# Splitting the Mamba layer's weights a chunk ahead, spreading dt's chain over Z, and letting DMA and TensorE take two products of the scan's core

## The chip, the cores and the metric

The program runs on one core of one Trainium2 chip. The metric is the device time in microseconds of one execution. Timed executions of the kernel before: 2147.05 us in the median of three (2145.24 to 2148.67).

## The reference

A stack of two layers over 256 latent tokens and 256 context tokens, width 1024, float32. Layer 0 mixes tokens with a Hyena long convolution, layer 1 with a bidirectional Mamba-2 scan; each mixer stands between two half-step SwiGLU feed-forward blocks. What the change touches is the Mamba mixer of layer 1:

```python
def project(h):
    zxbcdt = h @ in_w                       # z, x, B, C, dt side by side
    xbc = silu(dwconv_centered(xbc_part, conv_w, conv_b))     # 3 taps along the tokens
    dt = softplus(dt_part + dt_bias)
def ssd_chunked(xdt, da, bm, cm, init):     # per chunk of 128 tokens, per head
    a_cs = cumsum(a);  decay_in = exp(segsum(a))
    y_diag = einsum(cb, decay_in, x)
    states = ...                            # B^T (decay * x), carried over chunks
    y_off = einsum(cc, prev_states, exp(a_cs))
def finish(y, xs, z):
    y = (y + d_skip * xs) * silu(z)
    yg = y grouped in 8;  yg *= rsqrt(mean(yg^2) + EPS)
    return (yg * norm_w) @ out_w
```

Here `want_ctx` is false: the context tokens only supply the states with which the latent scan starts, in both directions. There are 32 heads of width 64 in 8 groups.

## The kernel before, in words

Channels lie on partitions, tokens on the free axis; latent and context tokens stand side by side (512 columns). Every weight product is done in three passes on TensorE (`mm3`, lines 1493 to 1495): high part of the weights by high part of the input, high by low, low by high. For that each 128x2048 chunk of weights is loaded to `raw[2]` (SyncE, `load`, line 411), its high part `wh[2]` is written by ScalarE (`split_hi`, line 558) and its low part `wl[2]` by VectorE (`split_lo`, line 883). Slots alternate: chunk n uses slot n % 2 of `wh` and `wl`, and its split waits until the chunk two before has been used (`w_used`); a raw slot is free when the low part of the chunk two before is done (`w_lo`).

The Mamba projection runs in this order. XB: 12 chunks of 256 channels for 512 tokens (x and B). DTP: one narrow chunk with dt, into bank 4. CP: 4 chunks for the 256 latent tokens (C). ZP: 8 chunks for the latent tokens (z). For XB and CP, `conv_chunk` (line 763) on ScalarE evicts two banks with the middle tap (line 770), VectorE adds the outer taps (`taps`, lines 1214 and 1216), ScalarE applies silu (line 776). In `conv_chunk` the split of the next chunk's weights comes first, then the wait for this chunk's matmuls, the evictions and the silus; so the following split stands behind these silus. In ZP the silu is the eviction (line 807). TensorE's waits between chunks are in `wide` (line 1763): `w_lo`, and banks free two chunks later; ZP waits for all of C's taps (line 1780).

dt's chain (softplus by a polynomial, cumulative sums, lines 1239 to 1294) is on VectorE: a first piece between DTP and CP (add, the 3.35 us reciprocal of line 1245), the rest in one block between CP and ZP, the last six small instructions after all of Z. Its results lie in `dts`, 64 partitions by 8 rows of 256, in the memory of `wh`/`wl`. ScalarE stores row 5 to `afscr` in HBM; SyncE reads it back, one head's two rows (forward and backward, 2 KB) broadcast to all partitions, into `afb[r]`.

After Z: TensorE turns B (`tb_mm`, line 1790), dt (line 1818) and the context's x (`turn_x`, line 1800); VectorE scales the turned x by rows of dt into `xtok` (line 1310); TensorE forms the states (line 1812); then the same turning for the latent x.

The core runs over 8 groups of 4 heads. ScalarE writes `csx[r] = exp(afb[r])` (line 840), GpSimd multiplies it by C (line 1480), ScalarE writes four 128-column exponentials into `ee[r]` (lines 844, 845, 849, 850), two of them from `dm`, which VectorE forms (`exponents`, lines 1333 and 1334); VectorE multiplies `ee[r]` by B.C (`products`, lines 1344 and 1345, semaphore `m_done`). TensorE adds the state part and four products for each pair of heads (lines 1864 to 1873), forms B.C of the next group (line 1839) and the sum of squares of the group two before (line 1847). VectorE gates a finished group (`gate_y`): two products with D (line 1357), then one with silu(z) (line 1361). ScalarE squares it (line 831) once `tt[2]` is free, which the sum of squares two groups before must release. Each engine takes this work in the order written in its block; only semaphores connect them. After the core come the group norm, the output product (MBOUT) and the last feed-forward block.

## Time and profile before

| What | Value |
|---|---|
| timed executions, median (lowest, highest) | 2147.05 us (2145.24, 2148.67) |
| profiled execution: time, and span from first to last instruction | 2147.36 us, 2145.5 us |
| TensorE busy, share of the span | 2001.8 us, 93% |
| VectorE, ScalarE, GpSimd busy | 1321.3, 686.0, 202.8 us |
| granted TensorE clock, mean | 0.971 |
| XB, one chunk on TensorE | 10.9 us |
| one tap of XB (128x510) / one modulation product (128x1024) on VectorE | 0.75 us / 1.2 us |
| raw weights of the Mamba projection, issue to landing, median | 5.4 us |
| issue of the two stores of dt's row (ScalarE's queue) | 0.8 us |

The slices of 2% of the span show TensorE at nine tenths nearly everywhere; the slices of the Mamba layer's middle are at seven and eight. A span is busy time, idle time that a wait ends, and matmuls at the lower clock level; the rows below show all three for the stretch from about 1510 to 1870 us, where the changed code runs.

### The profile page before, as it was taken

To read this page: it belongs to the slowest core of one execution; us is meant where nothing else is said; L and a number is where in the kernel's file an instruction comes from. 1 tells how busy PE (TensorE), PEld (TensorE's weight loads), DVE (VectorE), ACT (ScalarE), POOL (GpSimd) and SP (SyncE) were. 2 spreads that over 40 slices of the span, in tenths; PEclk is the share of its full clock that TensorE was granted. 3 is DMA by queue.
4 is the path that set the end of the run, shared out by engine and by line. 5 is a ranking of instruction groups with operands and counts; after the bars stand their busy time and mean duration, and the time that the engine had idled before them with its cause. 6 is when DMAs were issued, how large, how long until landed. Compare 5 with 4: busy or idle time off the path is not lost. (4 is left out here: it accounts for less than half of the span.)

```text
span 2145.5 us, 24954 instructions
## 1 busy us (share of the span) xinstructions
PE 2001.8 (93%) x10136; PEld 1672.0 (78%) x10136; DVE 1321.3 (62%) x1844; ACT 686.0 (32%) x913; POOL 202.8 (9%) x140
## 2 busy tenths in 40 slices
PE   5899999999989989999999999999899797698998
PEld 2688888878867868888887888888787784398998
DVE  6565546777857675554767565567765548845544
ACT  3422222232200232222224222222444335634442
POOL 1000000100023400000110000011000003340001
PEclk9999999999989999999999999999999898999999
DMA  8444435544520154442645444355432322444554
GB/s 322 152 159 155 137 106 183 165 139 135 179 76 1 41 165 148 139 155 83 201 153 171 138 152 143 104 173 165 147 118 89 118 84 74 123 133 152 186 155 141
DMA packets 274590, 298.25 MB, mean 139 GB/s; under 512 B 8912, under 2 KB 249136, under 8 KB 272688
## 3 DMA queue, kind: packets, MB, share of 16 engines
q1 hardware_dynamic: 270784, 285.44, 41.6%
q10 hardware_dynamic: 3696, 11.27, 1.4%
q8 instruction: 78, 1.28, 0.3%
q14 instruction: 32, 0.26, 0.0%
HBM read 290.31 MB, written 6.37 MB: 138 GB/s over the span
## 5 line engine op out<-in xcount | busy, mean ns | idle before, releaser
L1493 PE MATMUL banks<-xh,wh 128*128 128x512 f32 (+1 forms) x2120 | 782.3, 369 | 53.1 <-DVE xl L946 16.4
L1494 PE MATMUL banks<-xl,wh 128*128 128x512 f32 (+1 forms) x2120 | 777.0, 366 | 0.0
L1495 PE MATMUL banks<-xh,wl 128*128 128x512 f32 (+1 forms) x2120 | 776.4, 366 | 0.0
L883 DVE TENSOR_TENSOR wl<-raw,wh 128x2048 fp32r<-128x2048 f32 (+1 forms) x195 | 404.2, 2073 | 333.0 <-ACT wh L558 331.9
L558 ACT ACTIVATE wh<-raw 128x2048 fp32r<-128x2048 f32 (+1 forms) x201 | 349.6, 1739 | 644.6 <-PE banks L1495 562.9
L1493 PEld LDWEIGHTS banks<-xh,wh 128*128 128x128 f32 x2120 | 408.4, 193 | 124.5 <-issue 27.5
L1494 PEld LDWEIGHTS banks<-xl,wh 128*128 128x128 f32 x2120 | 408.4, 193 | 62.4
L1495 PEld LDWEIGHTS banks<-xh,wl 128*128 128x128 f32 x2120 | 407.8, 192 | 63.1
L1493 PE MATMUL banks<-gh,wh 128*128 128x512 f32 (+1 forms) x704 | 255.7, 363 | 2.9 <-DVE wl L883 1.6
L1494 PE MATMUL banks<-gl,wh 128*128 128x512 f32 (+1 forms) x704 | 255.2, 362 | 0.0
L1495 PE MATMUL banks<-gh,wl 128*128 128x512 f32 (+1 forms) x704 | 255.1, 362 | 0.0
L994 DVE TENSOR_TENSOR pp<-tt,banks 128x512 f32<-128x512 f32 (+1 forms) x88 | 50.7, 617 | 185.3 <-PE banks L1495 185.2
L1493 PEld LDWEIGHTS banks<-gh,wh 128*128 128x128 f32 x704 | 132.8, 189 | 24.5 <-DVE wl L883 2.2
L1494 PEld LDWEIGHTS banks<-gl,wh 128*128 128x128 f32 x704 | 132.8, 189 | 20.6
L1495 PEld LDWEIGHTS banks<-gh,wl 128*128 128x128 f32 x704 | 132.8, 189 | 20.4
L605 ACT ACTIVATE tt<-banks 128x512 f32<-128x512 f32 (+1 forms) x88 | 43.1, 542 | 271.0 <-PE banks L1495 271.0
L1430 POOL TENSOR_TENSOR acc<-acc,tt 128x512 f32<-128x512 f32 (+1 forms) x42 | 85.9, 2045 | 373.5 <-ACT tt L639 310.7
L1424 POOL MEMSET acc<- 128x512 f32 x6 | 3.2, 527 | 1176.0 <-DVE gl L974 931.4
L961 DVE SCALAR_TENSOR_TENSOR hT<-banks,mods,hT 128x256 f32<-128x256 f32 (+1 forms) x64 | 28.8, 481 | 108.2 <-PE banks L1495 108.2
L897 DVE SCALAR_TENSOR_TENSOR banks<-ada_rawo,cb 128x1024 f32<-128x1024 f32 x48 | 81.8, 1705 | 2.8 <-DMA ada_rawo<-in_ada_rest 2.8
L899 DVE SCALAR_TENSOR_TENSOR ada_rawf<-ada_rawf,cb 128x1024 f32<-128x1024 f32 x60 | 73.5, 1225 | 2.0
L897 DVE SCALAR_TENSOR_TENSOR banks<-ada_rawf,cb 128x1024 f32<-128x1024 f32 x60 | 73.7, 1228 | 0.0
(211 smaller groups left out, 1730.5 us busy)
## 6 DMA issues: line engine op xcount, KB each, us to landing
raw<-in_ffn_in SPq DMA_DIRECT2D x88, 1024.0 KB, 5.1
raw<-in_ffn_out SPq DMA_DIRECT2D x64, 704.0 KB, 4.8
ada_rawf<-in_ada_rest SPq DMA_DIRECT2D x60, 512.0 KB, 3.9
ada_rawo<-in_ada_rest SPq DMA_DIRECT2D x48, 512.0 KB, 4.0
raw<-in_mb_in_w SPq DMA_DIRECT2D x24, 1024.0 KB, 5.4
raw<-in_hy_in_w SPq DMA_DIRECT2D x12, 1024.0 KB, 5.2
afb<-decays SPq DMA_DIRECT2D x32, 256.0 KB, 3.1
raw<-in_mb_out_w SPq DMA_DIRECT2D x8, 1024.0 KB, 5.8
```

Source lines behind the costliest of these rows:

```text
L558: return act.activation(wh[n % 2][:, 0:cols], raw[r_slot][:, 0:cols], ACT.Copy).then_inc(w_hi, 1)
L605: act.activation(tt[u][:, 0:n], bank[u][:, 0:n], ACT.Silu).then_inc(gate_ready, 1)
L883: dve.tensor_tensor(wl[n_slot][:, 0:cols], raw[r_slot][:, 0:cols], wh[n_slot][:, 0:cols].bitcast(F32), ALU.subtract).then_inc(w_lo, 1)
L897: own(dve.scalar_tensor_tensor(banks[free][:].rearrange("p a n -> p (a n)"), pieces[i][:], half, cb0[:], ALU.mult, ALU.mult, accum_out=mod ...
L899: dve.scalar_tensor_tensor(pieces[i][:], pieces[i][:], half, c_ctx[:], ALU.mult, ALU.mult, accum_out=mods[layer][:, m, 1:2]).then_inc(ada_ ...
L961: ins = dve.scalar_tensor_tensor(x, bank[4 + um][:, w * L:w * L + L], mods[layer][:, i * 2 + (DT * k5 + um), w:w + 1], x, ALU.mult, ALU.add)
L994: dve.tensor_tensor(pp[(pi.q + u) % 2][:, 0:n], tt[u][:, 0:n], bank[2 + u][:, 0:n], ALU.mult).then_inc(p_ready, 1)
L1424: pool.memset(acc[:], 0.0).then_inc(acc_zero, 1)
L1430: pool.tensor_tensor(acc[:, 0:n], acc[:, 0:n], tt[um][:, 0:n], ALU.add).then_inc(acc_done, 1)
L1493: pe.matmul(dst, h, x_hi, start=start, stop=False)
L1494: pe.matmul(dst, h, x_lo, start=False, stop=False)
L1495: return pe.matmul(dst, l_, x_hi, start=False, stop=stop)
```

## The change

Splits: in XB, CP and ZP the split of chunk j+2 now comes right behind the evictions of chunk j, before the silus on ScalarE, and behind the taps of chunk j on VectorE (in XB before the modulation products). The waits for raw slots and for TensorE's banks are one chunk earlier to match; SyncE loads one chunk earlier at the joints between XB, DTP, CP and ZP. The loops of CP and ZP are written out.

dt: `dts` moves from the memory of `wh`/`wl` to that of `tt`, so that its rows may be written while Z's weights are in use. The chain is cut in pieces, which stand behind the low parts of ZP chunks 2 to 7. ScalarE's two exponentials and four stores stand behind the sixth eviction of Z; TensorE turns dt before ZP chunk 7.

After Z: TensorE turns x and B in mixed order.

Core: exp(af) is formed once for all heads by ScalarE (`dts` row 6), stored in `afscr[1]`, and SyncE loads it into `csx[r]` for each head, behind a wait for TensorE's use of the previous one (`cs_used`). ScalarE scales the latent x by D in place (`d_x`, `dx_done`), and TensorE adds it with an identity product per pair of heads; `gate_y` loses its two products with D.

The diff, cut to its core:

```diff
-        dts = at("dts", [P, 8, L], F32, o_w + 12 * KB)
+        dts = at("dts", [P, 8, L], F32, o_tt)
...
# SyncE
+            for j in range(4):
+                sp.wait_ge(w_lo, CP.w - 1 + j)
+                load(CP.raw + j, ...)
+            for j in range(8):
+                sp.wait_ge(w_lo, ZP.w - 1 + j)
+                load(ZP.raw + j, ...)
-            sp.wait_ge(af_st, 32)
+            sp.wait_ge(af_st, 64)
+            sp.wait_ge(tk_t, 1)
+            sp.wait_ge(w_used, ZP.w + 8)
             for g in range(GROUPS):
                 for r in range(HPG):
...
-                    sp.dma_start(afb[r][:], afscr[g * HPG + r].partition_broadcast(P)).then_inc(afb_in[r], 16)
+                    sp.dma_start(afb[r][:], afscr[0, g * HPG + r].partition_broadcast(P)).then_inc(afb_in[r], 16)
+                    if g:
+                        sp.wait_ge(cs_used, 2 * g - 1 + r // 2)
+                    elif r == 0:
+                        sp.wait_ge(dt_v, 4)
+                    sp.dma_start(csx[r][:].rearrange("p (a n) -> p a n", a=2),
+                                 afscr[1, g * HPG + r].partition_broadcast(P)).then_inc(cs_in[r], 16)
# ScalarE
-            def conv_chunk(pl, i, u, split, dst, n, t0):
+            def conv_chunk(pl, j, split, dst, n, t0):
+                act.wait_ge(w_used, pl.w + j + 1)
+                for s in range(2):
+                    ...  # evict with the middle tap
                 split()
...
+            def chunk_hi(pl, j, cols=CW):
+                r = pl.raw + j
+                split_hi((pl.w + j) % 2, cols, r % 2, r // 2 + 1, pl.w + j - 1)
+            for j in range(12):
+                conv_chunk(XB, j, lambda: (chunk_hi(XB, j + 2) if j < 10 else chunk_hi(DTP, 0, 8 * P) if j == 10
+                                           else chunk_hi(CP, 0)), lambda m: xb[:, :, m, :], NT, 0)
...
+            for j in range(8):
+                act.wait_ge(w_used, ZP.w + j + 1)
+                for s in range(2):
+                    act.activation(zsb[:, j * 2 + s, :], bank[2 * (j % 2) + s][:, 0:L], ACT.Silu).then_inc(z_free, 1)
+                if j < 6:
+                    chunk_hi(ZP, j + 2)
+                if j == 5:
+                    act.wait_ge(dt_v, 2)
+                    act.activation(dts[64:128, 4, :], dts[64:128, 3, :], ACT.Exp).then_inc(dt_e, 1)
+                    act.wait_ge(dt_v, 3)
+                    act.activation(dts[64:128, 6, :], dts[64:128, 5, :], ACT.Exp).then_inc(dt_e, 1)
+                    ...  # two stores of row 5, wait, two stores of row 6
...
+            def d_x(g):
+                for m in (2 * g, 2 * g + 1):
+                    act.activation(xb[:, 0, m, :], xb[:, 0, m, :], ACT.Copy, scale=dcol[:, m:m + 1]).then_inc(dx_done, 1)
+            act.wait_ge(tr_mm, 16)
+            d_x(0)
             for h in range(HEADS):
+                if r == 1 and g + 1 < GROUPS:
+                    d_x(g + 1)
-                act.activation(csx[r][:], afb[r][:].rearrange("p a n -> p (a n)"), ACT.Exp).then_inc(ex_done, 1)
# VectorE
+            for j in range(12):
+                for s in range(2):
+                    taps(XB, j // 2, j % 2, s, NT, 0)
+                if j < 10:
+                    chunk_lo(XB, j + 2)
...
+            chunk_lo(ZP, 2)
             own(dve.tensor_scalar(w, e, 2.0, None, ALU.add))
             own(dve.reciprocal(w, w))
+            chunk_lo(ZP, 3)
...              # three ops, polynomial terms 13 and 11
+            chunk_lo(ZP, 4)
...              # terms 9, 7, 5, 3, last product
+            chunk_lo(ZP, 5)
...              # dt, da, ones, two scans
+            chunk_lo(ZP, 6)
...              # rows 3, 0, 5, 1 of dts
+            chunk_lo(ZP, 7)
+                dve.tensor_tensor(zz, zz, bank[4 + (g - 1) % 2][:].rearrange("p (a n) -> p a n", a=2),
+                                  ALU.mult).then_inc(y_done, 1)
# GpSimd
-                pool.wait_ge(ex_done, h + 1)
+                pool.wait_ge(cs_in[r], 16 * g + 16)
# TensorE
+            for j in range(8):
+                pe.wait_ge(w_lo, ZP.w + j + 1)
+                ...  # bank free
+                if j == 7:
+                    pe.wait_ge(dt_v, 4)
+                    ...  # six transposes of dt
+                two_tiles((ZP.w + j) % 2, 2 * (j % 2), x0, n=L)
...
+            turn_x(0, 1, 0)
+            turn_b(0, 2)
+            turn_x(0, 1, 1)
+            turn_b(2, 4)
...
+                    m = 2 * g + p
+                    pe.wait_ge(dx_done, m + 1)
+                    pe.matmul(bank[4 + g % 2][:, p * L:p * L + L], ident, xb[:, 0, m, :], start=True, stop=False)
```

## Rows read from the trace of the kernel before

**Rows 1.** Stretches: length, busy us of PE, PEld, DVE, ACT, POOL, clock, DMA share, GB/s.

```profile
1655.00:1695.00 40.00, 28.80 (x203) 28.19 (x204) 24.26 (x29) 20.99 (x26) 0.00 (x0) 0.87 0.42 128
1695.00:1747.00 52.00, 48.02 (x375) 47.65 (x373) 22.95 (x19) 15.39 (x20) 0.00 (x0) 0.94 0.33 105
1747.00:1784.00 37.00, 28.23 (x151) 23.75 (x150) 23.16 (x45) 13.90 (x29) 3.81 (x3) 0.85 0.15 51
```

**Rows 2.** Timeline of TensorE, rows with idle time: start, duration, what, [idle, releaser].

```profile
1537.02 0.50 PE L1493 MATMUL banks<-xh,wh 128*128 128x512 f32 x1 [1.75 <-DVE wl L883]
...
1655.05 0.39 PE L1493 MATMUL banks<-xh,wh 128*128 128x256 f32 x1 [3.23 <-DVE wl L883]
1664.98 0.58 PE L1493 MATMUL banks<-xh,wh 128*128 128x256 f32 x1 [3.92 <-DVE wl L883]
...
1680.73 0.39 PE L1493 MATMUL banks<-xh,wh 128*128 128x256 f32 x1 [1.42 <-DVE wl L883]
...
1692.57 0.58 PE L1493 MATMUL banks<-xh,wh 128*128 128x256 f32 x1 [5.82 <-DVE tt L1216]
1704.99 0.58 PE L1493 MATMUL banks<-xh,wh 128*128 128x256 f32 x1 [3.98 <-DVE wl L883]
```

**Rows 3.** Timeline of ScalarE, then VectorE, at one chunk of C.

```profile
1673.59 1.02 ACT L770 ACTIVATE tt<-banks,vecs 128x256 f32<-128x256 f32 x2 [4.47 <-PE banks L1495]
...
1676.46 1.90 ACT L558 ACTIVATE wh<-raw 128x2048 fp32r<-128x2048 f32 x1
...
1678.39 2.29 DVE L883 TENSOR_TENSOR wl<-raw,wh 128x2048 fp32r<-128x2048 f32 x1 [2.29 <-ACT wh L558]
```

**Rows 4.** The same two timelines at chunks of Z.

```profile
1718.38 0.66 ACT L807 ACTIVATE zsb<-banks 128x256 f32 x2 [3.31 <-PE banks L1495]
1718.93 1.91 ACT L558 ACTIVATE wh<-raw 128x2048 fp32r<-128x2048 f32 x1
...
1720.87 2.29 DVE L883 TENSOR_TENSOR wl<-raw,wh 128x2048 fp32r<-128x2048 f32 x1 [3.47 <-ACT wh L558]
1726.63 2.29 DVE L883 TENSOR_TENSOR wl<-raw,wh 128x2048 fp32r<-128x2048 f32 x1 [3.47 <-ACT wh L558]
```

**Rows 5.** One group of the core (columns as rows 1), and the loads of afb.

```profile
1824.60:1834.40 9.80, 7.16 (x56) 3.86 (x56) 9.77 (x23) 7.38 (x22) 5.10 (x4) 1.00 0.35 110
DMA to landing us min/median/max: 3.0/3.1/4.5
```

**Rows 6.** The chain that ended last, one place of it a group apart.

```profile
1838.23 0.67 DVE mm L1344
...
1848.04 0.68 DVE mm L1344
```

**Rows 7.** Timeline of VectorE and ScalarE at dt's chain.

```profile
1659.15 3.35 DVE L1245 RECIPROCAL rs<-rs 64x512 f32<-64x512 f32 x1
1694.45 4.30 DVE L1263 SCALAR_TENSOR_TENSOR rs<-rs,tt 64x512 f32<-64x512 f32 x6
1656.58 1.28 ACT L791 ACT_TABLE_LOAD   x1 [3.91 <-DVE tt L1240]
```

**Rows 8.** Timeline of TensorE and VectorE between Z and the core.

```profile
1747.79 1.09 PE L1790 MATMUL banks<-small,xb 128*128 128x128 f32 x8 [0.75 <-ACT zsb L807]
...
1767.34 7.07 PE L1812 MATMUL banks<-xtok,btok 128*128 128x256 f32 x32
...
1774.96 9.66 DVE L1310 TENSOR_TENSOR xtok<-banks,tk 128x512 f32<-128x512 f32 x16 [4.32 <-PE banks L1800]
...
1784.67 2.07 PE L1839 MATMUL banks<-csb,xb 128*128 128x256 f32 x4 [3.77 <-DVE xtok L1310]
```

**Rows 9.** One line's instructions: count, duration ns min/median/max; and the last L1357.

```profile
L1333 DVE SCALAR_TENSOR_TENSOR dm<-afb,tkd x32: 339/572/998, 1769.5 to 1858.8; 128x128 f32<-128x128 f32 x32
L1361 DVE TENSOR_TENSOR zsb<-zsb,tt x8: 691/1005/1016, 1801.5 to 1866.4; 128x512 f32<-128x512 f32 x8
1865.45 0.87 DVE L1357 SCALAR_TENSOR_TENSOR tt<-xb,dcol,banks 128x256 f32<-128x256 f32 x2 [1.65 <-PE banks L1873]
```

More of the change, by code:

```diff
@@ L372, in build @@
         e_done = sem("e_done")
-        ex_done = sem("ex_done")
+        cs_in = [sem(f"cs_in{r}") for r in range(HPG)]
+        cs_used = sem("cs_used")
+        dx_done = sem("dx_done")
         cs_done = sem("cs_done")
@@ L773, in conv_chunk @@
-                for s in range(2):
-                    m = i * 4 + (u * 2 + s)
-                    act.wait_ge(conv_free, m + (pl.conv + 1))
+                    m = j * 2 + s
+                    act.wait_ge(conv_free, pl.conv + m + 1)
                     act.activation(dst(m), tt[t0 + s][:, 0:n] if n == L else
                                    tt[t0 + s][:].rearrange("p (a n) -> p a n", a=2), ACT.Silu).then_inc(cv_silu, 1)
-            def xb_pair(i, last):
-                for u in range(2):
-                    split = lambda: (split_hi(DTP.w, 8 * P, DTP.raw % 2, DTP.raw // 2 + 1, DTP.w - 1)
-                                     if last and u == 1 else next_hi(XB, i, u, 2) if i or u else None)
-                    conv_chunk(XB, i, u, split, lambda m: xb[:, :, m, :], NT, 0)
@@ L1245, in _ @@
             own(dve.reciprocal(w, w))
-            def c_pair(i, last):
-                for u in range(2):
-                    if last and u == 1:
-                        open_lo(ZP)
-                    else:
-                        next_lo(CP, i, u, 2)
-                    for s in range(2):
-                        taps(CP, i, u, s, L, 2)
-            steps(dve, 2, c_pair, own, 4)
-            z, z2, s_ = tt[0][hp, :], tt[1][hp, :], rs[hp, :]
+            chunk_lo(ZP, 3)
             own(dve.tensor_tensor(z, e, w, ALU.mult))
```

169 lines of the change are left out of this document (77 added, 92 removed).

## The prediction, made before the changed kernel was run

> **What bounds the kernel now.** I read the page first: TensorE is busy 93% of the span, so only stretches where it stands or runs slowly can give time back. The stretches of the Mamba layer [rows 1] show them: TensorE is busy 28.8 of 40 us in C (granted clock 0.87), 48.0 of 52 in Z (0.94), 28.2 of 37 in the turning and states part (0.85). TensorE's timeline, its rows with idle time before them [rows 2], then names the waits: 1.75 us at XB's third chunk, and in C and Z 3.23, 3.92, 1.42, 5.82 and 3.98 us, 18.4 together, all for VectorE (the low part of the weights four times, and once the last conv tap, L1216). After three of them a 128x256 matmul begins at 0.58 us instead of 0.39: the lower of the clock's two levels (1.2 against 2.4 GHz). Third, one chunk of C on ScalarE and VectorE [rows 3] shows why: eviction starts at 1673.59 and ends at 1674.61, but the split of the next weights starts at 1676.46, because the silus stand between and wait for the taps. The same places in Z [rows 4] have no silu between: chunk period 5.76 us, TensorE never idle. Last, the core: VectorE is busy 9.77 of 9.80 us [rows 5], and the chain of waits shows one loop of 9.81 us [rows 6].
>
> **XB.** The third chunk's low part no longer stands behind VectorE's first modulation product. New order: taps of chunk 0 until about 1527.4, low part 2.3 us to 1529.7; TensorE needs it at 1535.2. The 1.75 us wait goes; with the slower first matmul 1.9 us. The later chunks take 10.9 us on TensorE and had no waits; VectorE needs at most 0.8 (first eviction) + 3.0 (four taps) + 2.3 + 5.2 (four modulation products of 1.2 with their small reads), 11.3 of the 11.7 us until its next taps: covered by 0.4 us, and if that fails it eats the slack of the low part (over 4 us) first. The raw loads queue behind modulation loads on SyncE; weights land some 4 us before their split. Worth 1.9 us.
>
> **C and Z.** From the end of dt's matmuls (1655.05 - 3.23 = 1651.82) to the end of Z (1747.79 - 0.75 = 1747.04) are 95.2 us; twelve chunks at 5.76 are 69.1. What remains in the new order:
> - Start of C: last XB eviction, taps until 3.8 us after its start, low part 2.3: 6.1 us, against 5.3 us of dt matmuls. 0.9 us of wait remains, where there were 3.23.
> - In C, behind the end of a chunk: evictions 1.0 (0.9 before the next starts), high part 1.90, low part 2.29, handovers 0.15: 5.3 against 5.76 us [rows 3]. The four taps (1.9 us, from 0.6 on) end before the high part does. Cover 0.5 us. Silus and a 1.28 us table load fit behind the split on ScalarE.
> - In Z: 0.55 + 1.90 + 2.29 + 0.15 = 4.9 against 5.76 [rows 4]; cover 0.9 us.
> - dt's chain in pieces in Z's gaps on VectorE. The pieces: add and reciprocal 3.9 [rows 7]; three ops and two of the six polynomial steps (4.30/6 each) 3.3; four steps and one 3.6; five ops and scans 3.1; six small ops 2.1. With a low part of 2.3 these are 6.2, 5.6, 5.9, 5.4 and 4.4 in periods of 5.76. Added up in order, each low part still ends 0.3 to 0.6 us before TensorE wants it. This is the thinnest cover of the forecast: price if one piece is late, that lateness.
> - At Z's sixth eviction ScalarE takes two exponentials, four stores (0.4 each) and two table switches, 2 x 1.28 + 0.7 + 1.6 = 4.9 us. Queued behind: the silus of chunk 6, 2 us late. Nobody waits: chunk 7 uses the other banks, and the first turn into banks 0 and 1 comes 5.8 us later.
> - The six transposes before chunk 7 now lie on the path, 0.9 us (0.87 before, elsewhere on it).
> - Raw weights: a load is issued when the low part two chunks before ends; 5.4 us to land, 7.2 until the split. 1.8 us to spare.
> Sum 0.9 + 69.1 + 0.9 = 70.9; gain 24.3 us.
>
> A table switch stands in the trace as 1.28 us [rows 7], the exponential 0.02 us behind it. The Trainium skill (ScalarE: Activation LUTs, What ACT_TABLE_LOAD costs) counts 1.28 plus 1.38 us of drain for each switch and so speaks against two more of them in Z. By it the first exponential is 1.4 us later, dt's last product too, and TensorE waits about 0.9 us before chunk 7: gain 23.4 instead of 24.3.
>
> **Turning and states.** Now 37.6 us from 1747.04 to 1784.67. On the path: eight transposes 1.04 to 1.09 [rows 8], four such groups 4.2, then the last btok copy 0.7; four rounds of states at 3.5 (7.07 for two) with two more groups 2.1, 16.1; VectorE's sixteen products 9.66 with 0.7 before them. New: 4.9 + 16.1 + 10.4 = 31.4. The order gives 6.2 us: VectorE's first products start 1 us behind Z (8 us now), dt's tail and transposes are gone from here, and the slow transposes (16 in 3.7 us) with the waits that precede them. If the clock falls here anyway, 2 to 3 us of it are lost. SyncE's eight loads (4 row pairs, 4 exponentials) start at Z's end and must be there 16 us later: hidden. The scaling with D (ScalarE, after transpose 16) is done about 3 us before the core starts.
>
> **Core.** VectorE loses the two products with D (0.87 for both), ScalarE the 512-wide exponential (0.52 a head, 2.1 a group) against two copies with scale (0.7), TensorE gets two identity products (0.5 each). Yet the loop [rows 6] does not contain the products with D: products of head r=1 done, four rounds of TensorE (1.45), next B.C (1.06), sum of squares (0.97), square on ScalarE (0.7 with the handover), two exponentials, products of head 3: 5.0 us; then VectorE's products and exponents of heads 3, 0, 1: 3.9 us, and 0.9 us of stretching. That stretching is L1333, 0.34 us at least, 0.57 in the median, 1.00 at most [rows 9], each time while GpSimd's 1.27 us product runs. L1361, also with both inputs in SBUF, shows 0.69 to 1.02. In the new kernel GpSimd starts when its DMA lands, by my sum while VectorE is in its slack half of the loop; I take the 0.9 off. TensorE's extra 0.53 ahead of the pair puts it 0.25 us behind VectorE. New loop 9.81 - 0.9 + 0.25 = 9.15; seven intervals give 4.6. Bounds for the loop: 8.9 (TensorE not late) and 9.8 (stretching stays, its extra hidden). After the last head the products with D are on the path: 0.9. Together 5.5.
>
> **Loads in the core.** The four loads of a group become eight of 256 KB. Four keep the DMA engines busy 35% of 9.8 us [rows 5], 0.86 us each; eight are 6.9 of 9.15 us. One lands 3.1 us after issue, 4.5 where four were issued together. New on SyncE: each exponential's load waits for TensorE (cs_used), and the next head's row pair is queued behind it. The tightest is head 3's row pair: it now leaves 9.6 us into the loop, lands 12.7 to 14.1, and VectorE wants it at 12.9 with 1.4 us of slack. Hidden, just.
>
> **Sum.** 1.9 + 24.3 + 6.2 + 5.5 = 37.9. The profiled execution took 2147.36 (span 2145.5), 0.3 over the median: 2109.5 for it, 2109.2 for the median.
>
> **Rivals.**
> - The core keeps its 9.8 us: the loads let GpSimd collide with L1333 in the half of the loop without slack, or head 3's row pair is late. For: the stretching took 0.9 us in every group before, and the slack is thin. Against: by my times the collision moves. 2109.2 + 4.6 = 2113.8 (2112 to 2116). The Trainium skill (GPSIMD Engine Reference, Specifications) has GpSimd's SBUF interfaces shared with VectorE and colliding with VectorE instructions that have two SBUF inputs. L1333 keeps its two and GpSimd its 32 products, so that rule stands behind this rival; the rows of L1333 and L1361 agree with it.
> - Weights late in C and Z. For: covers of 0.3 to 0.6 us. If VectorE's pieces are 0.5 us longer, 3 to 4 us go in waits; and if such waits bring the lower clock at one or two chunks, 2.8 each (8.5 against 5.76): 2114 to 2121.
> - The loads bind the core in part: 1.1 us for each further load in a burst, (1.8 + 4.5 - 3.0)/3, makes eight 8.8 us, and with SyncE waiting in order 10 to 12: seven times 1 to 3, 2116 to 2130.
> - Slower than before: the row loads run one after another because SyncE's queue waits on cs_used between them. Gains outside the loop are 33.3 us, so it decides from 9.8 + 33.3/7 = 14.6 us a group, 1.8 us a load; at the full 3.1 us it would be 24.8 a group, 2220. Against: 4 loads landed within 6.3 us of the first issue.
> - Better: loop 8.9, C's first wait hidden, products of group 1 quicker: 2101 to 2104.
>
> **Chances.** Forecast 0.54 (own range 2104 to 2113), core unchanged 0.17, weights late 0.11, loads bind in part 0.08, slower 0.03, better 0.07. Range 2102 to 2121: the first three and half of the last. A change of 0.2%, 4.3 us, is what a measurement of this kernel can tell from none. Faster 0.95, same 0.02 (between the third and the fourth rival), slower 0.03.
>
> **What would show it.** C and Z: TensorE's waits between dt and the end of Z below 2 us, granted clock 1.00, twelve chunk starts 5.76 apart. VectorE's first xtok product about 1 us behind Z; core start 31.4 behind Z. In the core: distance of L1344 of head 3 from group to group 9.15, L1333 mostly at 0.34, TensorE's waits for m_done small. The prediction is wrong if low parts end after the chunk before them, if GpSimd's products still stretch L1333 on the loop, if SyncE's issues of row pairs come later than 10 us into a loop, or if the clock of the states part stays at 0.85.

## The result and the profile after

| | before | after |
|---|---|---|
| median of four executions | 2147.86 us (2145.24 to 2148.76) | 2110.43 us (2109.44 to 2111.57) |
| ratio, 95% interval | | 0.9834 [0.9819, 0.9849] |
| profiled execution, span | 2147.36, 2145.5 | 2109.44, 2107.6 |
| mean granted clock | 0.971 | 0.976 |

The changed kernel is 1.7% faster: 37.4 us by the medians, 37.9 by the two spans. The forecast was 2109.2 and a gain of 37.9. (The median of the kernel before, 2147.86, is that of four executions; the section on the chip has that of three of them.) The stretches of the Mamba layer in the changed kernel come first; the columns are those of [rows 1]: C with Z, turning and states, core.

```profile
1648.30:1718.90 70.60, 69.97 (x583) 69.77 (x584) 51.30 (x57) 37.75 (x49) 0.00 (x0) 1.00 0.50 151
1718.90:1749.30 30.40, 24.27 (x145) 20.81 (x143) 20.55 (x36) 11.17 (x22) 5.07 (x4) 0.92 0.24 77
1749.30:1836.30 87.00, 69.93 (x480) 37.15 (x480) 71.43 (x158) 52.40 (x149) 35.91 (x28) 0.93 0.66 194
```

Three numbers of the first row answer the forecast for C and Z: length 70.6 us (70.9), TensorE busy in nearly all of it, clock 1.00, where [rows 1] had 0.87 and 0.94. TensorE's timeline says the same; these are its rows with idle time from the start of XB to the core:

```profile
1509.22 0.77 PE L1511 MATMUL banks<-xh,wh 128*128 128x512 f32 x1 [2.91 <-DVE xl L967]
...
1522.87 0.50 PE L1511 MATMUL banks<-xh,wh 128*128 128x512 f32 x1 [0.53 <-DVE wl L953]
...
1648.93 0.39 PE L1511 MATMUL banks<-xh,wh 128*128 128x256 f32 x1 [0.64 <-DVE wl L904]
...
1723.24 3.72 PE L1847 MATMUL banks<-xtok,btok 128*128 128x256 f32 x16 [0.69 <-ACT btok L833]
...
1749.33 1.22 PE L1872 MATMUL banks<-csb,xb 128*128 128x256 f32 x2 [3.71 <-DVE xtok L1332]
```

The five waits of C and Z [rows 2], 18.4 us, have become one of 0.64, where 0.9 was forecast. XB's wait of 1.75 us is gone. The 0.53 us before XB's second chunk stood in the kernel before too (0.54).

Z's last matmul ends at 1719.0 (before at 1747.04). With it the 37.9 us between the spans divide so:

| part | before | after | gain | forecast |
|---|---|---|---|---|
| up to XB's first matmul (code not changed) | 1510.42 | 1509.22 | 1.2 | 0 |
| XB, dt, C, Z | 236.6 | 209.8 | 26.8 | 26.2 |
| turning and states | 37.6 | 30.3 | 7.3 | 6.2 |
| core, to the first matmul of the normalization | 88.8 | 87.0 | 1.8 | 5.5 |
| the rest | | | 0.7 | 0 |

So the sum fitted partly because errors cancelled: the core gave a third of what it was to give, and small gains elsewhere stood in for the missing 3.7: 0.6 and 1.1 more than forecast in the two parts above it, and 1.2 and 0.7 in code that wasn't changed.

**The core.** TensorE takes the four heads of a group in two pairs, p=0 and p=1. A loop is the distance from one start of p=1's products (first round L1904) to the next. The rows are p=1 and p=0 in turn, and the idle time in brackets is TensorE waiting for VectorE's products:

```profile
1779.37 0.65 PE L1904 MATMUL banks<-mm,xtok 128*64 128x256 f32 x4 [0.83 <-DVE mm L1367]
...
1782.74 0.65 PE L1904 MATMUL banks<-mm,xtok 128*64 128x256 f32 x4 [0.21 <-DVE mm L1367]
...
1788.76 0.65 PE L1904 MATMUL banks<-mm,xtok 128*64 128x256 f32 x4 [0.83 <-DVE mm L1367]
...
1792.69 0.65 PE L1904 MATMUL banks<-mm,xtok 128*64 128x256 f32 x4 [0.77 <-DVE mm L1367]
...
1798.70 0.65 PE L1904 MATMUL banks<-mm,xtok 128*64 128x256 f32 x4 [0.83 <-DVE mm L1367]
...
1803.61 0.65 PE L1904 MATMUL banks<-mm,xtok 128*64 128x256 f32 x4 [1.74 <-DVE mm L1367]
...
1809.63 0.65 PE L1904 MATMUL banks<-mm,xtok 128*64 128x256 f32 x4 [0.83 <-DVE mm L1367]
...
1812.76 0.65 PE L1904 MATMUL banks<-mm,xtok 128*64 128x256 f32 x4
...
1818.78 0.65 PE L1904 MATMUL banks<-mm,xtok 128*64 128x256 f32 x4 [0.83 <-DVE mm L1367]
```

These loops take 9.39, 9.94, 10.93 and 9.15 us (all seven: 8.47, 9.61, 9.39, 9.94, 10.93, 9.15, 8.53). The forecast's 9.15 is there where p=0 doesn't wait; the others are longer by p=0's wait of 0.21, 0.77 and 1.74 us. One place shows where such a wait comes from; VectorE (DVE) and GpSimd (POOL) side by side:

```profile
1788.62 0.35 DVE L1355 SCALAR_TENSOR_TENSOR dm<-afb,tkd 128x128 f32<-128x128 f32 x1
1788.70 1.41 POOL L1498 TENSOR_TENSOR tt<-tt,csb 128x512 f32<-128x512 f32 x1 [1.23 <-DMA tt<-decays]
1788.88 1.37 DVE L1356 SCALAR_TENSOR_TENSOR dm<-afb,tkd 128x128 f32<-128x128 f32 x1
1790.18 0.68 DVE L1366 TENSOR_TENSOR mm<-ee,banks 128x512 f32<-128x512 f32 x1
```

GpSimd's product starts as soon as its load has landed. The exponent instruction behind it (L1356, 0.34 us by itself) lasts 1.37 and ends at 1790.25, 0.14 after GpSimd's 1790.11. The product L1366, which reads one input from PSUM, is not stretched: 13 of the 32 run beside a GpSimd product, and none of the 32 takes over 0.69 us. The other two loops have such cases as well:

```profile
1779.23 0.81 DVE L1355 SCALAR_TENSOR_TENSOR dm<-afb,tkd 128x128 f32<-128x128 f32 x1
...
1798.57 1.33 DVE L1355 SCALAR_TENSOR_TENSOR dm<-afb,tkd 128x128 f32<-128x128 f32 x1
...
1801.28 1.35 DVE L1356 SCALAR_TENSOR_TENSOR dm<-afb,tkd 128x128 f32<-128x128 f32 x1
```

Between p=1's start, or just before it, and p=0's products the exponents are stretched by 0.47, 1.03 and 2.00 us in the three long loops (what 0.81, 1.37, and 1.33 with 1.35 have over 0.34), and TensorE's wait is 0.26 us less each time: that is the 0.25 us by which the forecast had TensorE behind VectorE. In the loop of 9.15 nothing is stretched there. The same sum, 9.15 and what the stretching exceeds 0.26 by, gives the four middle loops of this kernel and of three more below (quarter loads, split behind the silus, dt in one block), sixteen in all, within 0.04 us.

The groups of the exponents in the core, first before (L1333, L1334), then after (L1355, L1356):

```profile
L1333 DVE SCALAR_TENSOR_TENSOR dm<-afb,tkd 128x128 f32<-128x128 f32 x30 | 16.7, 557 | 0.0
...
L1334 DVE SCALAR_TENSOR_TENSOR dm<-afb,tkd 128x128 f32<-128x128 f32 x30 | 11.3, 376 | 0.0
```

```profile
L1355 DVE SCALAR_TENSOR_TENSOR dm<-afb,tkd 128x128 f32<-128x128 f32 x30 | 16.0, 532 | 2.7 <-DMA afb<-decays 2.6
L1356 DVE SCALAR_TENSOR_TENSOR dm<-afb,tkd 128x128 f32<-128x128 f32 x30 | 12.3, 410 | 0.0
```

Sixty instructions at 0.34 us are 20.4 us. Stretching of the exponents was 7.6 us before (16.7 + 11.3 - 20.4) and is 7.9 now, and 9.4 and 11.6 in two later kernels with the same code in the core: nothing of it went. It only changed form, fewer cases and longer ones: over 0.5 us 18 before and 12 after, over 1 us one (L1334, 1.40) and five. What did go is the stretching of the gate: L1361, with both inputs in SBUF, took 0.99 to 1.02 us in the seven cases beside a GpSimd product and 0.69 in the one without; L1378, which reads PSUM, takes 0.67 to 0.69 in all eight. New are 2.6 us of waits for row pairs. ScalarE's waits and the loads in the core:

```profile
ACT tt L846 <- PE banks L1880: 19.2, 7, 3.7
...
ACT ee L865 <- DMA afb<-decays: 3.0, 3, 1.4
```

```profile
afb<-decays SPq DMA_DIRECT2D x28, 256.0 KB, 4.7
```

The first row is the square of each group waiting for TensorE's sum of squares of the group before. A row pair lands 4.7 us after its issue where it was 3.1.

### The profile page after: what moved, and what is told of

Read it like the earlier page. It is cut to its first block and busy times, and to the rows that moved or that the text cites. A ratio compares the mean times of both kernels' runs of the same rounds, so it can differ in the third digit from the quotient of the medians.

```text
span 2107.6 us, 24932 instructions
## 1 busy us (share of the span) xinstructions
PE 1999.1 (95%) x10168; PEld 1667.9 (79%) x10168; DVE 1312.2 (62%) x1828; ACT 677.1 (32%) x899; POOL 203.0 (10%) x140
## 5 line engine op out<-in xcount | busy, mean ns | idle before, releaser
L1512 PEld LDWEIGHTS banks<-gl,wh 128*128 128x128 f32 x704 | 132.9, 189 | 20.4
```

The lines of the kernel that those rows point to most:

```text
L1512: pe.matmul(dst, h, x_lo, start=False, stop=False)
```

## Experiments

Each kernel is the changed kernel with the edit shown; each ratio is to the kernel before, run on the same chip. The first four ran on one chip, the next four on another, the last four on a third. Medians of before there: 2146.12, 2144.57 and 2145.11 us. The core falls into three parts: the start up to p=1's first products, the seven loops, and the end from p=1's last start to the norm. "Low until" is how long the granted clock stays at its lower level from the core's start on; "stretching" is that of the exponents.

| kernel | core | start | low until | seven loops | end | stretching |
|---|---|---|---|---|---|---|
| before | 88.8 | 12.0 | 9.0 | 67.2 | 9.6 | 7.6 |
| changed | 87.0 | 12.0 | 9.0 | 66.0 | 9.0 | 7.9 |
| exponentials back on ScalarE | 88.8 | 10.4 | 5.1 | 69.3 | 9.1 | 10.9 |
| D back on VectorE | 92.1 | 12.1 | 9.3 | 70.3 | 9.7 | 10.5 |
| both back | 89.1 | 12.2 | 9.5 | 67.2 | 9.7 | 7.6 |
| quarter loads | 85.1 | 10.5 | 5.2 | 65.6 | 9.0 | 6.5 |
| two square tiles | 85.1 | 10.4 | 5.3 | 65.9 | 8.7 | 11.6 |
| small product | 83.3 | 12.0 | 9.0 | 62.3 | 9.0 | 0.4 |
| squares and quarter loads | 82.1 | 10.4 | 5.1 | 62.9 | 8.7 | 9.0 |
| squares and row order | 85.6 | 12.2 | 9.4 | 64.6 | 8.8 | 13.7 |
| squares and gate | 81.7 | 10.5 | 5.1 | 62.5 | 8.7 | 6.9 |
| squares, order and gate | 81.0 | 12.1 | 9.4 | 60.0 | 8.8 | 9.9 |
| split behind silu (core as changed) | 87.6 | 10.5 | 4.2 | 68.1 | 9.1 | 11.6 |
| dt in one block (core as changed) | 86.4 | 10.4 | 5.1 | 67.0 | 9.0 | 9.4 |

Two things follow. The start takes 12.0 to 12.2 us or 10.4 to 10.5, with the clock low for 9.0 to 9.5 us or for 4.2 to 5.3; it doesn't follow the edits, so 1.5 us of a difference between two cores can be the clock alone. And the loops of three kernels with the same code in the core are 66.0, 67.0 and 68.1 us. (The two kernels with the old core repeat each other, 67.2 and 67.2.) So edits are compared by their loops, and a difference under 2 us there says nothing by itself.

Theories for the missing 3.7 us: **A**, the loop runs through sum of squares and square, and GpSimd's products stretch VectorE on it; **B**, eight loads a group, some queued behind TensorE, hold it back; **C**, VectorE's busy time bounds it. The expectations go by the core's whole length.

**Exponentials back on ScalarE.**

```diff
 # SyncE
-                    ...  # its wait for cs_used
-                    sp.dma_start(csx[r][:]..., afscr[1, g * HPG + r].partition_broadcast(P)).then_inc(cs_in[r], 16)
 # ScalarE
+                    act.wait_ge(head_mm, h - 3)
+                act.activation(csx[r][:], afb[r][:].rearrange("p a n -> p (a n)"), ACT.Exp).then_inc(ex_done, 1)
 # GpSimd
-                pool.wait_ge(cs_in[r], 16 * g + 16)
+                pool.wait_ge(ex_done, h + 1)
```

> Undoes one part of the core: the 512-wide exponential is again written by ScalarE from afb and GpSimd waits for it; SyncE loads only the four row pairs of a group (the two extra stores stay). Splits, dt's chain, turning and D on TensorE stay as changed. The core is measured from the first B.C matmul (L1872 in the changed kernel) to the first matmul of the group norm's broadcast: 88.9 us before, 87.0 after, 83.4 by my sum. Theory A (the loop through the sum of squares stays at 5.0 us, and GpSimd's products stretch VectorE's L1355 and L1356 on it, whoever releases them): the core is 86 to 88 us, the time within 2 us of the changed kernel's 2110.4. Theory B (eight loads of 256 KB a group hold the core back): the core falls to about 84 us, time about 2107.

Measured 2113.79 us, 0.9849 [0.9823, 0.9876]; core 88.8 us, row pairs land after 3.2 us again. That is outside both expectations: B's gain doesn't come, and A's 86 to 88 us and its 2 us around 2110.4 are missed too. The loops are 69.3 us, four of them 10.6, where the kernel before had 9.8. D on TensorE alone makes the loops 2.1 us longer than neither piece does (67.2, before and with both back), and only the short start hides it; the end is 0.6 us shorter.

**D back on VectorE.**

```diff
 # ScalarE
-            d_x(0)
-                    d_x(g + 1)
 # VectorE, gate_y
+                for mt in range(2):
+                    own.mark(dve.scalar_tensor_tensor(tt[3][...], xb[:, 0, m, :], dcol[:, m:m + 1], bank[4 + (g - 1) % 2][...],
+                                                      ALU.mult, ALU.add))
 # TensorE
-                    pe.matmul(bank[4 + g % 2][:, p * L:p * L + L], ident, xb[:, 0, m, :], start=True, stop=False)
```

> Undoes the other part of the core: the products with D are again two VectorE instructions in gate_y, no copies with scale on ScalarE and no identity products on TensorE; exponentials still by DMA. Theory A (the products with D are off the loop except behind the last group, where they cost 0.9 us; TensorE's identity product puts it 0.25 us behind on the loop): core 87 to 89 us, time 2110 to 2113. Theory C (VectorE's busy time bounds the core): the core goes up by 8 times 0.9, to 94 us, time about 2117.

Measured 2115.82 us, 0.9859 [0.9834, 0.9884]; core 92.1 us, VectorE busy 82.32 of it, granted clock 0.87 (0.93 in the changed kernel). It lies between the two expectations. The loops are 70.3 us: exponentials by DMA without D on TensorE are 3.1 us worse than neither piece.

**Both back.** The two diffs above together.

> Both parts of the core's change are undone (exponentials on ScalarE, products with D on VectorE); projections, dt's chain, turning and states stay as changed. If the core of the changed kernel is only worth what the two traces differ by (1.8 us), the core is 88.8 us and the time 2112.2 (2111.5 to 2113). If one half of the core's change needs the other (exponentials by DMA alone cost 5.1 by the run with D on VectorE, D on TensorE alone left the core at 88.8), the core stays between 88.5 and 92. If the other parts of the change had given the core something, it is below 88: 2111 or less.

Measured 2112.4 us, 0.9852 [0.9835, 0.9868]; core 89.1 us. As expected, this is the core of the kernel before. The two pieces together are worth 2.1 us here (1.8 by the traces of before and after): 1.2 in the loops, 0.6 to 0.7 at the end, the rest in the start. The 1.2 isn't clear of what the same code varies by (loops of 66.0 to 68.1 us against 67.2). Each piece alone makes the loops longer.

**Loads of the exponentials cut to a quarter.**

```diff
-                    sp.dma_start(csx[r][:]..., afscr[1, g * HPG + r].partition_broadcast(P)).then_inc(cs_in[r], 16)
+                    q = 64 if g else L
+                    sp.dma_start(csx[r][:]...[:, :, 0:q], afscr[1, g * HPG + r, :, 0:q].partition_broadcast(P)).then_inc(cs_in[r], 16)
```

> From the second group on the exponentials' loads bring 64 of each 256 columns (64 KB for 256 KB), with the same waits and order; the other columns are multiplied again in place, so the output is not the reference's. Theory B (bytes in flight hold the core back: row pairs land in 4.7 us in the median, 3.1 before): landing falls to about 3.2 us, VectorE's waits for afb go, core about 84 us, time about 2107. Theory A (what stretches the loop is GpSimd's product, not the landing): landing falls as well, but the core stays at 86 to 88 us.

Measured 2109.84 us, 0.983 [0.9807, 0.9853]; core 85.1 us. DMA share 0.45 (0.66 in the changed kernel), row pairs land after 4.0 us and cost VectorE 0.7 us and ScalarE 0.9 us of waits (2.6 and 3.0 in the changed kernel), and exponent instructions still reach 1.37. Of the 1.9 us that the core is shorter 1.5 are the start, where the clock rose earlier. The loops are 65.6 us, 0.4 below the changed kernel and 1.3 below the nearest other kernel with its code. By itself B isn't shown to be worth anything.

**Two tiles for the square.**

```diff
-                if g > 1:
-                    act.wait_ge(g_sum, g - 1)
-                act.activation(tt[2][:], ...Square)
+                if g > 2:
+                    act.wait_ge(g_sum, g - 2)
+                act.activation(tt[2 + (g - 1) % 2][:], ...Square)
```

> The square of a gated group goes to tt[2] and tt[3] in turn, and ScalarE waits for the sum of squares one group later than now; nothing else changes. Theory A (the core's loop runs through the sum of squares on TensorE and the square on ScalarE): the loop opens, ScalarE no longer waits 2 to 3 us before a square, the group falls from 9.4 us to 8.6 to 8.9, bounded by TensorE's work (8.1 us) and by VectorE's (7.5 plus stretching); core 82 to 84 us, time 2105 to 2107. Theory B (loads): no change, 2110.

Measured 2106.72 us, 0.9819 [0.9791, 0.9846]; core 85.1 us, where A wanted 82 to 84. Its waits of ScalarE:

```profile
ACT ee L870 <- DVE dm L1356: 15.1, 20, 2.8
ACT tt L846 <- DVE zsb L1378: 11.4, 8, 3.9
```

The square no longer waits for TensorE, only for its own input, and instead the exponentials wait for VectorE's exponents, 20 times where it was 11. Taking the square out of the loop made VectorE the next in line, with 17.7 + 14.3 - 20.4 = 11.6 us of stretching. That is as much as one of the kernels with the core as changed has, so that VectorE collides more by this edit isn't shown. The core's 1.9 us are 1.5 of start and 0.3 of end; the loops are the changed kernel's (65.9 against 66.0). The interval of the ratio overlaps that of the changed kernel.

**GpSimd's product nearly left out.**

```diff
-                pool.tensor_tensor(cs, cs, csb[:, g, :].unsqueeze(1).to_broadcast([P, 2, L]), ALU.mult).then_inc(cs_done, 1)
+                pool.tensor_tensor(cs[:, :, 0:16], cs[:, :, 0:16], csb[:, g, 0:16].unsqueeze(1).to_broadcast([P, 2, 16]), ALU.mult).then_inc(cs_done, 1)
```

> GpSimd's product of the exponential with C works on 16 of 256 columns in each half, so it leaves most of the product out (the rest of the operand is the exponential alone); everything else as in the changed kernel. Theory A (the loop through the sum of squares and the square, stretched by GpSimd's products): VectorE's exponent instructions lose the stretched cases (maximum below 0.6 us instead of 1.43), core 84 to 85 us instead of 87.0, time 2107.5 to 2108.5. Theory B (the eight loads hold the core back): stretched instructions go, but the waits for row pairs stay or grow by as much; core 86.5 to 87, time 2110 to 2110.5. Theory C (VectorE's busy time bounds): the whole 0.9 us of each of seven loops, core 81 to 82, time 2105 to 2106.

Measured 2105.17 us, 0.9811 [0.9795, 0.9828]. The core's window, its groups of exponents, and the starts of p=1 (here L1905):

```profile
1748.60:1831.90 83.30, 69.61 (x480) 37.17 (x480) 64.34 (x158) 52.04 (x149) 7.30 (x28) 0.93 0.71 203
```

```profile
L1355 DVE SCALAR_TENSOR_TENSOR dm<-afb,tkd 128x128 f32<-128x128 f32 x30 | 10.4, 347 | 4.3 <-DMA afb<-decays 4.3
L1356 DVE SCALAR_TENSOR_TENSOR dm<-afb,tkd 128x128 f32<-128x128 f32 x30 | 10.4, 345 | 0.0
```

```profile
1787.53 0.65 PE L1905 MATMUL banks<-mm,xtok 128*64 128x256 f32 x4 [0.83 <-DVE mm L1367]
...
1796.68 0.65 PE L1905 MATMUL banks<-mm,xtok 128*64 128x256 f32 x4 [0.83 <-DVE mm L1367]
...
1805.83 0.65 PE L1905 MATMUL banks<-mm,xtok 128*64 128x256 f32 x4 [0.83 <-DVE mm L1367]
```

No instruction is stretched, the four middle loops are 9.15 us to the hundredth, the core 83.3 us: the forecast's 9.15 and 83.3 (88.8 less 5.5). The start is that of the changed kernel, so all 3.7 us come from the loops (62.3 against 66.0): 2.8 in the three long loops above, 0.6 in the last one, where TensorE had waited 0.42 us for VectorE and 0.90 for a GpSimd product, and 0.3 in the first two. The loads are as in the changed kernel (DMA share 0.71, waits for row pairs 4.3 us) and cost nothing here. The core is shorter than A's 84 to 85 and longer than C's 81 to 82, and the time would fit C (2105 to 2106). What speaks against C is that VectorE is busy only 30.85 of the 36.60 us of these four loops. The loop's pieces by the chain of waits and the timeline: TensorE's two pairs with the next B.C and the sum of squares 6.7 us, square and two exponentials 1.3, VectorE's products of one head 1.15.

**Squares and quarter loads together.** Both edits above.

> Two tiles for the square in turn, and the loads of the exponentials cut to a quarter of their columns from group 1 on (the operand then holds old values in the rest, so part of the data is wrong in kind but the work on the engines is the same). Each alone gave a core of 85.1 us from 87.0. Theory A and B both true and independent: 83.2 to 83.6, time about 2106.5. If both lead to the same limit (VectorE's busy time with its stretched instructions): 85 us, time 2108.

The kernel leaves out what the quarter loads leave out. Measured 2107.64 us, 0.9827 [0.9808, 0.9846]; core 82.1 us, below the 83.2 to 83.6 expected. Here the smaller loads do shorten the loops: 62.9 us, 2.7 and 3.0 below either edit alone, with the same start. The median shows nothing of it against the kernel with two tiles (ratio 0.9819): its four executions lie between 2103.06 and 2110.17, the profiled one at 2105.33.

**Squares, and SyncE's row pairs ahead of the wait for TensorE.**

```diff
 # SyncE, per pair of heads
+                for p in range(2):
+                    for r in (2 * p, 2 * p + 1):
...
+                        sp.dma_start(afb[r][:], afscr[0, g * HPG + r].partition_broadcast(P)).then_inc(afb_in[r], 16)
+                    if g:
+                        sp.wait_ge(cs_used, 2 * g - 1 + p)
...
+                    for r in (2 * p, 2 * p + 1):
+                        sp.dma_start(csx[r][:]..., afscr[1, g * HPG + r].partition_broadcast(P)).then_inc(cs_in[r], 16)
```

> Two tiles for the square in turn, and SyncE issues both row pairs of a pair of heads before it waits for TensorE to have used the exponentials, so that no row pair stands behind that wait. Theory B in the form 'order of the queue': the waits for row pairs (2.4 and 1.6 us in the run with two tiles) go, core 83.5 to 84.5, time 2105.5 to 2107. Theory B in the form 'bandwidth of eight loads': waits stay, core 85, time 2107. The row pair's landing tells them apart: near 3 us in the first, 4.5 or more in the second.

Measured 2112.62 us, 0.9856 [0.984, 0.9872]; core 85.6 us. Row pairs land after 3.9 us (4.7), and neither VectorE nor ScalarE waits for one. The core's length doesn't fall, but only because the start is 1.7 us longer (12.2 against 10.4, clock low until 9.4 instead of 5.3); the loops are 64.6 us, 1.3 below those with two tiles alone, which is within what the same code varies by. VectorE is busy 76.4 us (74.7), and stretching is 17.3 + 16.8 - 20.4 = 13.7 us with 13 instructions above 1 us, the most of any kernel here: at least a part of the waits removed was turned into collisions. Of the two forms of B the order of the queue was right about the waits and the landing; its gain of 1 us or so in the core can't be told from none. The profiled execution took 2108.38, the other three more; what made them longer isn't in a trace.

**Squares, and GpSimd waits for the exponents of its head.**

```diff
                 pool.wait_ge(cs_in[r], 16 * g + 16)
+                pool.wait_ge(d_done, h + 1)
```

> Two tiles for the square in turn, as in the run before with two tiles (core 85.1), and GpSimd also waits until VectorE has made the exponents of the same head, so that its 1.27 us product starts beside VectorE's two products from PSUM (1.08 us) and not beside an exponent instruction. Theory A (GpSimd's products stretch VectorE's exponent instructions, on the loop): stretched cases above 1 us go, VectorE's busy time in the core falls from 74.7 to 68 to 70 us, core 82.5 to 84, time 2104 to 2106. Rival: the loads land later than the exponents are made, so the wait changes nothing in the order: core 85, 2107. Other side: the products are late for TensorE: core above 85.5.

Measured 2106.13 us, 0.982 [0.9803, 0.9838]; core 81.7 us, VectorE busy 70.1. One wait more for GpSimd takes 3.4 us off a core of 85.1, all of it in the loops (62.5 against 65.9): its groups of exponents are 17.1 and 10.2 us, stretching 6.9 where it was 11.6, and one instruction is above 1 us (1.02) where there were eight. The core is shorter than A's 82.5 to 84; VectorE's 70.1 and the time lie 0.1 us outside A's ranges. VectorE's waits for row pairs (4.5 us) are still there. The time by the median does not follow the core by that much (the profiled execution took 2103.76).

**The same with the row order.**

> The same wait of GpSimd, in the kernel with two tiles for the square and SyncE's row pairs ahead of the wait for TensorE (core 85.6, VectorE busy 76.4). Theory A: with the rows there in time, only the collisions were left of that core; VectorE's busy time falls to 69 to 71 us, core 81.5 to 83.5, time 2102.5 to 2105. If the core stays at 85 to 86 with the collisions gone, the row order costs by the loads of the exponentials coming later, and TensorE waits for GpSimd's products.

Measured 2103.72 us (2102.21 to 2104.71), 0.9804 [0.9787, 0.9822]:

```profile
1749.40:1830.40 81.00, 70.46 (x481) 37.27 (x481) 72.57 (x158) 52.05 (x148) 38.40 (x30) 0.92 0.68 209
```

```profile
L1357 DVE SCALAR_TENSOR_TENSOR dm<-afb,tkd 128x128 f32<-128x128 f32 x30 | 18.1, 605 | 0.0
...
L1358 DVE SCALAR_TENSOR_TENSOR dm<-afb,tkd 128x128 f32<-128x128 f32 x30 | 12.2, 408 | 0.0
```

```profile
1787.81 0.68 DVE L1368 TENSOR_TENSOR mm<-ee,banks 128x512 f32<-128x512 f32 x1
1788.03 1.28 POOL L1501 TENSOR_TENSOR tt<-tt,csb 128x512 f32<-128x512 f32 x1 [1.08 <-DVE dm L1358]
1788.40 0.41 DVE L1369 TENSOR_TENSOR mm<-ee,banks 128x256 f32<-128x256 f32 x1
1788.74 0.72 DVE L1357 SCALAR_TENSOR_TENSOR dm<-afb,tkd 128x128 f32<-128x128 f32 x1
```

The timeline shows what the wait does: GpSimd starts at 1788.03, beside the two products that read PSUM, and when the exponent L1357 comes only 0.57 us of its 1.28 are left; the exponent is stretched to 0.72, not 1.37. It doesn't do so everywhere: eight instructions are still above 1 us (13 without the wait), and stretching is 9.9 us (18.1 + 12.2 - 20.4; it was 13.7). The core is 81.0 us, 4.6 less than the same kernel without the wait, all of it in the loops (60.0 against 64.6); TensorE's waits for VectorE's products are 4.3 us instead of 10.6. The core is below the 81.5 to 83.5 expected, and VectorE's busy time, 72.6 us, misses the 69 to 71. This is the fastest kernel of the study: 41.4 us below before, where the change alone gave 37.4. Its interval (up to 0.9822) touches that of the changed kernel (from 0.9819), so the difference of the two times, about 6 us, rests on the medians and on the loops in the traces (60.0 against 66.0 to 68.1), not on a comparison on one chip.

**In C, the split behind the silus.**

```diff
-                split()
+                if n != L:
+                    split()
                 for s in range(2):
...
                     act.activation(dst(m), tt[t0 + s][:, 0:n]..., ACT.Silu).then_inc(cv_silu, 1)
+                if n == L:
+                    split()
```

> In C alone ScalarE splits the next weights behind the two silus again, as before the change; everything else as changed. Theory of the forecast (the split behind an eviction is late because the silus wait for the taps): the high part starts about 1.9 us later after each C chunk, the chain behind an eviction is 7.2 us against 5.76, so TensorE waits about 1.4 us at four chunks, 5.6 us, and 2.8 more where a wait brings the lower clock: end of Z 5.6 to 8.4 us later, time 2116 to 2119. Rival: the order on ScalarE was worth little, and the gain came from the weights being split a chunk further ahead on VectorE: below 2113.

Measured 2113.01 us, 0.9843 [0.9823, 0.9864]; core starts 3.3 us later (1752.6). TensorE's rows with idle time in C and behind it:

```profile
1648.11 0.39 PE L1514 MATMUL banks<-xh,wh 128*128 128x256 f32 x1 [0.64 <-DVE wl L907]
...
1661.40 0.39 PE L1514 MATMUL banks<-xh,wh 128*128 128x256 f32 x1 [1.52 <-DVE wl L907]
...
1667.81 0.39 PE L1514 MATMUL banks<-xh,wh 128*128 128x256 f32 x1 [0.40 <-DVE wl L907]
...
1674.60 0.38 PE L1514 MATMUL banks<-xh,wh 128*128 128x256 f32 x1 [0.77 <-DVE wl L907]
...
1681.01 0.39 PE L1514 MATMUL banks<-xh,wh 128*128 128x256 f32 x1 [0.40 <-DVE wl L907]
```

The first wait is in the changed kernel too. The other four, at the four chunks whose split was moved, are 3.1 us together, where the forecast's theory had 1.4 each. The clock stays at 1.00. Between 1646 and 1720 TensorE is busy 70.27 of 74.00 us, against 73.36 in the changed kernel: the same 3.1 us. The mechanism is there, at about half the size I gave it, and no lower clock comes with it; the time is below the theory's 2116 to 2119 and at the rival's bound (2113).

**dt's chain in one block.**

```diff
-            chunk_lo(ZP, 2)
             dve.wait_ge(dt_e, 2)
             own(dve.tensor_scalar(w, e, 2.0, None, ALU.add))
             own(dve.reciprocal(w, w))
-            chunk_lo(ZP, 3)
...
+            dve.wait_ge(cv_silu, 2 + 32)
...
+            chunk_lo(ZP, 2)
+            chunk_lo(ZP, 3)
+            chunk_lo(ZP, 4)
+            chunk_lo(ZP, 5)
+            chunk_lo(ZP, 6)
             chunk_lo(ZP, 7)
```

> dt's chain on VectorE (reciprocal, polynomial, scans, small differences: 16 us by the terms of the forecast) stands in one block ahead of Z's third low part, instead of in five pieces; everything else as changed. Theory of the forecast (only the cutting into pieces hides it): the third low part comes 16 us less its slack of 3.5 late, TensorE waits 12 to 13 us once, and 1 to 3 more for the clock after it: time 2122 to 2126. Rival: what hides the chain is that it stands inside Z at all, where VectorE has slack, and the wait is below 6 us: 2111 to 2117.

All five pieces stand ahead of the third low part. (At the added wait, for C's last silu, VectorE stands 0.11 us.) Measured 2125.06 us, 0.9902 [0.9883, 0.992]; core starts at 1763.8, 14.5 us later.

```profile
1695.84 0.58 PE L1512 MATMUL banks<-xh,wh 128*128 128x256 f32 x1 [11.99 <-DVE wl L904]
```

One wait of 11.99 us, a first matmul at the lower clock (0.58 against 0.39), and 2.5 us more behind it: as the forecast's theory had it. What hides dt's chain is that it is cut.

## Why the prediction was right, and the step that was not

**XB and the weights: held.** C, Z and XB gave 26.8 us against 26.2: wait at the start of C 0.64 (0.9), chunks 5.76 apart, clock 1.00, no low part late. Of these 26.8, the cutting of dt's chain carries 14.5 and the order of ScalarE in C 3.1, each undone by itself. The rest was not tried singly. The thin covers (0.3 to 0.6 us a period) held.

**The table switches: held.** ScalarE at Z's sixth eviction:

```profile
1709.31 1.28 ACT L820 ACT_TABLE_LOAD   x1
1710.61 0.42 ACT L820 ACTIVATE dts<-dts 64x256 f32<-64x256 f32 x1
...
1712.17 1.28 ACT L815 ACT_TABLE_LOAD   x1 [0.84 <-ACT dts L822]
1713.46 0.66 ACT L815 ACTIVATE zsb<-banks 128x256 f32<-128x256 f32 x2
```

The exponential starts 0.02 us behind a load of 1.28, the silu 0.01. The first load itself starts 0.01 us behind the split of weights before it, and the 0.84 us before the second are the issue of two stores (0.78). The drain of 1.38 us that the Trainium skill (ScalarE: Activation LUTs, What ACT_TABLE_LOAD costs) adds to each switch isn't in these rows, and TensorE waits nowhere before chunk 7: the trace decides for the 1.28 alone.

**Turning and states: 7.3 against 6.2.** VectorE's sixteen products take the 9.66 us of the forecast:

```profile
1719.48 4.87 DVE L1332 TENSOR_TENSOR xtok<-banks,tk 128x512 f32<-128x512 f32 x8 [5.56 <-PE banks L1835]
...
1739.62 9.66 DVE L1332 TENSOR_TENSOR xtok<-banks,tk 128x512 f32<-128x512 f32 x16 [4.32 <-PE banks L1835]
```

VectorE's first product is 0.5 us behind Z (1 forecast), the states start 4.2 us behind it (4.9), and their rounds took 15.7 (16.1) at a clock of 1.00; the clock falls only behind them (0.92 for the whole stretch, 0.85 before).

**Core: 1.8 against 5.5, the step that failed.** The sum had "I take the 0.9 off", because GpSimd would start when its DMA lands, in the half of the loop where VectorE has slack. It doesn't stay there: beside the starts of p=1 at 1779.37, 1788.76, 1798.70 and 1809.63 GpSimd's nearest product begins 0.75, 0.06, 0.22 and 1.67 us earlier, and the stretching of the exponents is 7.9 us as before (7.6). The seven loops gave 1.2 us where 4.6 were forecast, the products with D behind the last head 0.6 where it was 0.9. Leave most of GpSimd's product out and the core is 83.3 us with a loop of 9.15, which are the forecast's own numbers. So the rest of the core's working held (D off VectorE, the identity products on TensorE), and the missing 3.7 us are GpSimd's products on the loop. The forecast also read the stretching from L1333 alone, "1.00 at most"; L1334 beside it had reached 1.40. The case was on the list as the first rival, at 0.17, with the core unchanged, and one of the forecast's own signs of being wrong came true (GpSimd's products still stretch the exponents on the loop). What came is most of that rival: 1.8 us of core gained where it had 0.9, and with the same code the loops of two other kernels are 67.0 and 68.1 us against 67.2 before. That the total lies 1.2 us from the forecast is luck to that extent: a kernel with loops of 68.1 us would have come out at about 2112.5, an estimate from the median and these loops. The Trainium skill (SBUF — State Buffer, Who interferes with whom) has VectorE and GpSimd take a shared port pair as an exclusive lock, so that the second to start waits for the first; the rows above agree with it: L1356 ends 0.14 us behind GpSimd's product.

**Loads: half right.** "Hidden, just" was too kind. The eight loads landed after 4.7 us instead of 3.1, row pairs were waited for (2.6 us on VectorE), and cutting them took 3.0 us off the loops with two tiles for the square, but only 0.4 by itself, which is not clear of none. Without GpSimd's products the same waits cost nothing, and the sixteen loops above need no term for the loads. What the loads do decide is when GpSimd starts, and so whether it collides; stretching fell with the smaller ones both times (7.9 to 6.5 and 11.6 to 9.0 us). Why they land at other places from group to group stays open.

**Open too:** why each of the core's two pieces by itself makes the loops longer (69.3 and 70.3 us against 67.2), and why the clock rises earlier in some cores than in others. With D left on VectorE the clock also falls three times within the loops, for 3.4 us each, the only kernel here where it does; whether that is cause or consequence wasn't told apart.

## What to carry to other kernels

Where an engine's instructions are stretched by another's, letting a DMA's landing set the other's start didn't take the collision off the path here: count it as kept, unless a wait pins the start beside work that doesn't collide. Here that wait, one line on GpSimd, was worth 3.4 and 4.6 us of the core, more than both of the change's pieces there. When a wait in a loop is removed, look which engine is next, and what it will collide with: the earlier row pairs took VectorE's waits away and brought the most stretching of all. Cut a stretch into its loops before comparing two kernels: 1.5 us of the core's length here was the clock at its start, as much as some edits seemed to give. And check a sum by its parts even when the total fits.

## What the runs showed of the hardware

- VectorE's exponent instruction (two inputs in SBUF) lasts 0.34 us alone and up to 1.43 beside a GpSimd product of 1.27; with the product cut to 0.25 us, all 64 lie between 0.342 and 0.353. Instructions with one input in PSUM (L1366, 0.67 to 0.69) aren't stretched.
- It works the other way too: the GpSimd product that started 0.08 us behind L1355 took 1.41 instead of 1.27.
- Row pairs (broadcast loads of 256 KB) land after 3.1 to 3.2 us with four loads a group (DMA share 0.36) and after 4.7 with eight (0.66), 3.9 to 4.1 with eight in the other order (0.64 to 0.68); with the exponentials' at 64 KB, 4.0.
- The same code took 1.5 us longer at the core's start where the granted clock stayed at its lower level for 9.0 to 9.5 us instead of 4.2 to 5.3.
- A table switch took 1.28 us of ScalarE in Z, and the next instruction began 0.01 to 0.02 us behind it.
